# Moving the tiles of a float32r kernel within SBUF: moving tiles at one place modulo 512, gate and up weights 192 bytes below it

## What is computed

```python
def _swiglu(h, w_gate, w_up, w_down):
    return (jax.nn.silu(h @ w_gate) * (h @ w_up)) @ w_down     # 1024 -> 2816 -> 1024

x = x + 0.5 * _swiglu(_rmsnorm(x, g[0]), ffn_w_gate[layer, 0], ffn_w_up[layer, 0], ffn_w_down[layer, 0])
...
x = x + 0.5 * _swiglu(_rmsnorm(x, g[2]), ffn_w_gate[layer, 1], ffn_w_up[layer, 1], ffn_w_down[layer, 1])
```

## The kernel before

| tile | role | before | changed |
|---|---|---|---|
| `w_hi`, `w_lo`, `w_raw`, `xT`, `R` | weights of down and mixer products; state | 320 | 320 |
| `ffn_aH`, `ffn_aL` | moving, down products | 320 | 320 |
| `hH`, `hL` | moving, gate-up and mixer products | 64 | 320 |
| `st_hi`, `st_lo` | moving, gate-up | 448 | 320 |
| `tmp`, `ident`, `ones`, `bones` | scratch and constants | 448 | 320 |
| `gu_w_hi` 0, 1 | weights, gate-up | 384, 0 | 128, 128 |
| `gu_w_lo` 0, 1, 2 | weights, gate-up | 256, 384, 0 | 320, 128, 128 |
| `mixH`, `mixL`, `mH`, `mL`, `o_hi`, `o_lo`, `cq_hi`, `cv_hi` and other mixer tiles | moving | 64 | 320 |
| `yH`, `yL` and others of the first block | moving | 0 | 256 |
| `par`, `small` | columns of parameters | 320, 128 | 128, 224 |

## Time and profile before

### The profile page before, as it was taken

The page is one execution under the profiler, slowest core; times in us unless marked ns, Lnnn a source line. Parts: engine busy times, 40 slices in busy tenths (PEclk is TensorE's granted clock), DMA queues, the critical chain, the costliest instruction groups (busy, mean ns, idle before and its releaser), DMA issues.

```text
span 2411.5 us, 42260 instructions
## 1 busy us (share of the span) xinstructions
PE 2339.2 (97%) x16963; PEld 1986.4 (82%) x16963; DVE 1738.6 (72%) x2296; ACT 1144.1 (47%) x1758; POOL 880.0 (36%) x533
## 2 busy tenths in 40 slices
PE   8999989999999999988999999999999999999999
PEld 6667768789899777876898998998987557898997
DVE  7999986496486489765874867856856776883871
ACT  5533353465364346244662654643644344662552
POOL 3799944322313456422114133132134212114123
PEclk9999999999999999999999999999999999999999
DMA  5222214233343432002334343342333221233333
GB/s 151 79 79 79 75 57 127 74 88 100 104 115 90 111 90 74 27 3 58 111 95 118 106 114 89 88 131 77 114 88 100 52 58 53 81 101 107 106 89 96
DMA packets 420791, 214.48 MB, mean 89 GB/s; under 512 B 17317, under 2 KB 419035, under 8 KB 420603
## 3 DMA queue, kind: packets, MB, share of 16 engines
q1 hardware_dynamic: 416523, 209.05, 30.6%
q10 hardware_dynamic: 4080, 2.83, 0.5%
HBM read 209.22 MB, written 2.10 MB: 88 GB/s over the span
## 4 chain that ended last, share of the span: by engine, by line
PE 73%; DVE 17%; issue 3%; ACT 3%; POOL 3%; DMA 0%; ACTq 0%; DVEq 0%; POOLq 0%
PE bank L995 10%; PE bank L1000 10%; PE bank L1003 10%; PE bank L344 9%; PE bank L341 9%; PE bank L337 9%; DVE bank L1690 4%; PE bank L1863 2%; PE bank L1860 2%; PE bank L1856 2%; DVE gu_w_lo L592 1%; POOL w_lo L319 1%; PE bank L3400 1%; PE bank L2748 1%; DVE hL L368 1%
## 5 line engine op out<-in xcount | busy, mean ns | idle before, releaser
L319 POOL TENSOR_TENSOR w_lo<-w_raw,w_hi 128x1024 fp32r<-128x1024 f32 (+5 forms) x276 | 532.9, 1932 | 613.1 <-ACT w_hi L311 611.3
L311 ACT ACTIVATE w_hi<-w_raw 128x1024 fp32r<-128x1024 f32 (+5 forms) x276 | 237.6, 861 | 623.2 <-PE bank L344 468.7
L592 DVE TENSOR_TENSOR gu_w_lo<-gu_w,gu_w_hi 128x1024 fp32r<-128x1024 f32 (+1 forms) x256 | 364.9, 1428 | 90.6 <-ACT gu_w_hi L583 90.0
L664 POOL TENSOR_TENSOR ffn_aL<-tmp,ffn_aH 128x512 fp32r<-128x512 f32 x88 | 134.5, 1529 | 725.7 <-ACT ffn_aH L708 725.7
L583 ACT ACTIVATE gu_w_hi<-gu_w 128x1024 fp32r<-128x1024 f32 (+1 forms) x256 | 302.9, 1185 | 3.1 <-DVE gu_w L566 3.1
L995 PE MATMUL bank<-hH,gu_w_hi 128*128 128x256 f32 x1280 | 203.7, 281 | 5.0 <-ACT tmp L700 5.0
L1000 PE MATMUL bank<-hL,gu_w_hi 128*128 128x256 f32 x1280 | 200.7, 279 | 0.0
L1003 PE MATMUL bank<-hH,gu_w_lo 128*128 128x256 f32 x1280 | 200.3, 278 | 0.0
L700 ACT ACTIVATE tmp<-bank 128x256 f32<-128x256 f32 x320 | 120.8, 378 | 165.7 <-PE bank L1003 165.7
L968 DVE TENSOR_TENSOR bank<-bank,R 128x512 f32<-128x512 f32 x64 | 44.8, 699 | 204.1 <-PE bank L344 203.6
L337 PE MATMUL bank<-ffn_aH,w_hi 128*128 128x512 f32 x704 | 181.1, 390 | 0.0
(11 more groups left out here) (553 smaller groups left out, 4684.6 us busy)
## 6 DMA issues: line engine op xcount, KB each, us to landing
gu_w<-in_ffn_w_gate SPq DMA_DIRECT2D x88, 512.0 KB, 3.7
gu_w<-in_ffn_w_up SPq DMA_DIRECT2D x88, 512.0 KB, 4.8
w_raw<-in_w_in SPq DMA_DIRECT2D x48, 512.0 KB, 3.8
w_raw<-in_ffn_w_down SPq DMA_DIRECT2D x64, 384.0 KB, 3.4
w_raw<-in_ffn_w_down SPq DMA_DIRECT2D x64, 320.0 KB, 3.2
w_raw<-in_even_w_in SPq DMA_DIRECT2D x26, 512.0 KB, 3.9
w_raw<-in_w_conv_out SPq DMA_DIRECT2D x8, 512.0 KB, 3.9
w_raw<-in_w_out SPq DMA_DIRECT2D x8, 512.0 KB, 3.9
```

Source lines behind the costliest of these rows:

```text
L311: nc.scalar.activation(w_hi[u % 2][:, 0:K, :], w_raw[u % 4][:, 0:K, :], ACT.Identity).then_inc(w_hi_ready, 1)
L319: nc.gpsimd.tensor_tensor(w_lo[u % 2][:, 0:K, :], w_raw[u % 4][:, 0:K, :], w_hi[u % 2][:, 0:K, :].bitcast(F32), ALU.subtract).then_inc(w_l ...
L592: nc.vector.tensor_tensor(gu_wl[v % 3][:, b0:b1, :, :], gu_w[v % 3][:, b0:b1, :, :], gu_wh[v % 2][:, b0:b1, :, :].bitcast(F32), ALU.subtra ...
L664: nc.gpsimd.tensor_tensor(aL[:, in_half(n), :], up_t[:, :], aH[:, in_half(n), :].bitcast(F32), ALU.subtract).then_inc(a_lo, 1)
```

## The change

Only addresses change. Every engine's list of instructions is the same, in the same order, with the same shapes and waits (9941 rows over all engines when repeated ones are merged). `par` and `small` go to the front, so that `xT` starts at 320 and everything from `tmp` to `hH` follows without a gap; `place` always works modulo 512; the gate and up weights are put 192 bytes below the moving tiles instead of 64; `gu_w` 0 follows `hL` directly and so lies at the moving tiles' own place; `gu_w_hi` 0 is put ahead of the `st` tiles.

```diff
-            def place(self, r, step=256):
+            def place(self, r):
-                self.at += (r - self.at) % step
+                self.at += (r - self.at) % 512
                 return self.at
...
-        small = m.put("small", [P, 8])
-        m.place(64)
+        par = Map(m.at).put("par", [P, 408])
+        small = Map(m.at + 4 * 408).put("small", [P, 8])
+        m.at += 4 * 416
+        m.place(320)
         xT = m.put("xT", [P, DT, T])
...
-        par = m.put("par", [P, 416])
...
-        hH_at = m.place(ring_at)
-        GU_PLACE = hH_at - 64
+        hH_at = m.at
+        GU_PLACE = hH_at - 192
         hH = m.put("hH", [P, DT, T], F32R)
...
-        u_at = [f_map.place(GU_PLACE), 0, Map(ring_at).place(GU_PLACE)]
+        u_at = [f_map.at, 0, Map(ring_at).place(GU_PLACE)]
         f_map.put("gu_room0", [P, 7, 4, P])
-        f_map.place(hH_at)
         aH = f_map.put("ffn_aH", [P, GU, T], F32R)
         aL = f_map.put("ffn_aL", [P, GU, T], F32R)
-        u_at[1] = f_map.place(GU_PLACE, 128)
+        u_at[1] = f_map.place(GU_PLACE)
         f_map.put("gu_room1", [P, 7, 4, P])
...
+        gu_wh0 = f_map.put("gu_w_hi0", [P, 7, 4, P], F32R)
+        f_map.place(hH_at)
...
-        f_hi_at = f_map.place(hH_at, 128)
+        f_hi_at = f_map.at
```

More of the change, by code:

```diff
@@ L404, in build @@
         f_map = Map(ARENA)
-        u_at = [f_map.place(GU_PLACE), 0, Map(ring_at).place(GU_PLACE)]
+        u_at = [f_map.at, 0, Map(ring_at).place(GU_PLACE)]
         f_map.put("gu_room0", [P, 7, 4, P])
-        f_map.place(hH_at)
         aH = f_map.put("ffn_aH", [P, GU, T], F32R)
         aL = f_map.put("ffn_aL", [P, GU, T], F32R)
-        u_at[1] = f_map.place(GU_PLACE, 128)
+        u_at[1] = f_map.place(GU_PLACE)
         f_map.put("gu_room1", [P, 7, 4, P])
-        gu_w = [Map(at).put(f"gu_w{i}", [P, 7, 4, P]) for i, at in enumerate(u_at)]
-        gu_wl = [Map(at).put(f"gu_w_lo{i}", [P, 7, 4, P], F32R) for i, at in enumerate(u_at)]
-        gu_wh = [f_map.put("gu_w_hi0", [P, 7, 4, P], F32R), Map(Map(ring_hi_at).place(GU_PLACE)).put("gu_w_hi1", [P, 7, 4, P], F32R)]
+        gu_wh0 = f_map.put("gu_w_hi0", [P, 7, 4, P], F32R)
+        f_map.place(hH_at)
         st_hi, st_f, st_lo = [], [], []
-        f_hi_at = f_map.place(hH_at, 128)
+        f_hi_at = f_map.at
         for k in range(4):
@@ L425, in build @@
             st_f.append(f_lo_map.put(f"st_f{k}", [P, 3, HT]))
+        gu_w = [Map(at).put(f"gu_w{i}", [P, 7, 4, P]) for i, at in enumerate(u_at)]
+        gu_wl = [Map(at).put(f"gu_w_lo{i}", [P, 7, 4, P], F32R) for i, at in enumerate(u_at)]
+        gu_wh = [gu_wh0, Map(Map(ring_hi_at).place(GU_PLACE)).put("gu_w_hi1", [P, 7, 4, P], F32R)]
         hLf = Map(hH_at + 4 * DT * T).put("hL_f", [P, DT, T])
```

## The result

The changed kernel takes 2421.55 us (median of 6 runs, 2419.51 to 2426.09), the kernel before beside it 2412.06 (2410.85 to 2414.3): a ratio of 1.0035 with a 95% interval of 1.0025 to 1.0046. It is slower by 9.5 us. The prediction was 2393, a gain. What happened is rival 1 in the main, which had been priced at 2419.5.

A forecast was written before the change was run, and what follows sets the result against it. TensorE's pitch was taken to bound the kernel. Gain 21.7 - 0.8 - 1.7 = 19.2 us, giving 2394.1 from the profiled execution and 2392.4 from the median; predicted 2393 us, range 2389 to 2408.

The forecast's parts named there:

- rival 1: 256-wide gate-up matmuls: the slow pace is never shed, all 6720 run slow, 29.6 us instead of 21.7; 2419.5 us, chance 0.13.
- What bounds the kernel: Whole kernel: TensorE's pitch, busy 97% of the span; in second halves a mean of 116.6 ns from two paces.
- At constant places the pace persists: Gate-up units: with weights and moving operand at unchanged places, either pace (113.3 or 117.7 ns) continues; distance alone doesn't set it.
- The sum of the pace's cost, 21.7 us: All 256-wide matmuls: windows less their matmuls at 113.33 ns, 12.0 + 9.8, about 21.7 us to be gained before deductions.
- A change of the moving tile's place ends the fast pace: Borders of hH and st: the event, four times in a unit's seven products, would be gone with one moving place.
- The slow start of each of eight halves, until something ends it: 24 matmuls: Start of each feed-forward half: 24 matmuls slow by 4.4 ns, 0.1 us each, 0.8 us off the gain.
- Distance 0, bounds 0 and 3.3 us, taken at 1.7: Low-weight rounds of units v = 0, 3, 6, 9: between no cost and slow pace, half taken, 1.7 us off the gain.
- Rival 2: Units with low weights at distance 0 are slow throughout, the next without it fast again; 10.0 us stay, 2400.7 us, chance 0.20.
- There is room: Second halves: VectorE's 87.8 us fit into 104.7 us, 84%; the coming unit's low weights, next to be late, have room.
- Rival 4: VectorE or ScalarE takes the gain: ring of copies from PSUM binds, half the gain lost at most; 2402 us, chance 0.03.
- Plain units, mixer and down products unchanged: 512-wide matmuls: plain units taken at 0, bounds -1 and +1 us; mixer and down products keep their distance modulo 256, cost nothing.
- The rule of the SBUF — State Buffer page: TensorE's two independent read ports: a tile's place can't matter, sum 0, 2411.6 us; the prediction held the two paces against it.

The follow-up runs named there:

- run 1: Changed kernel with low buffer 0 at distance 64 too, so all gate and up weights at 64 from the one moving place: 2417.92 us.
- run 9: Changed kernel with all five weight buffers at distance 64 and the gated product earlier on VectorE: 2414.22 us, ratio 1.0006 to the kernel before.
- run 10: Changed kernel with all five weight buffers at distance 192 and the gated product earlier on VectorE: 2418.62 us, ratio 1.0023 to the kernel before.
- run 4: Changed kernel with the state sums (st tiles) alone 128 bytes off, so two moving places: 2412.15 us, ratio 1.0 to the kernel before.
- run 11: Changed kernel with high weights at distance 192, low ones at 64, and the gated product earlier on VectorE: 2395.67 us, ratio 0.9925 to the kernel before.
- run 8: Changed kernel with all five gate and up weight buffers at distance 0 from the one moving place: 2435.8 us, ratio 1.0097 to the kernel before.
- run 2: Changed kernel with one moving place kept but weights at the distances of the kernel before (high 64, 192; low 192, 64, 192): 2407.61 us.
- run 3: Changed kernel with both high weight buffers at distance 192 and all three low ones at 64: 2415.82 us, ratio 1.0015 to the kernel before.
- run 5: One moving place, weights at the distances of the kernel before, plus the gated product earlier on VectorE: 2391.09 us, ratio 0.991 to the kernel before.

## Why the prediction was wrong

- **What bounds the kernel: right.** The whole result lies in TensorE's pitch. Pace cost and gaps explain 8.6 of 9.5 us.
- **"At constant places the pace persists": right**, and too right. With all distances equal it persisted slow for 924 matmuls (runs 1, 9 and 10) and fast for 672 (run 9, units 69 to 76).
- **The sum of the pace's cost, 21.7 us: some 2.4 too high.** By the pitches the same windows hold 19.3 us of slow pace. The rest is mostly gaps between matmuls that the busy time of TensorE does not show, above all in the windows of 7 and 9 units (1.4 and 1.7 us of slow pace where I had 2.5 and 2.7).
- **"A change of the moving tile's place ends the fast pace": half of it.** The other half is that a step of the moving tile can also start the fast pace, where it takes the distance from 192 to 64 (run 4, and the counts there). This row was before me: the 12 matmuls on hH after st in unit 37 were fast after two or three, and no weight buffer changed its place there. I booked the event as a loss only. The change removes the loss and the cure.
- **"The slow start of each of eight halves, until something ends it: 24 matmuls", 0.8 us: the step that failed.** In the four second halves nothing in the changed kernel ends it: they are slow for all of their 924 matmuls, 4.3 us each where the term had 0.1. Run 1 shows the same without distance 0, and runs 9 and 11 show what was missing, a distance that goes from 192 to 64. With the first halves, the pace cost of the whole 256-wide work was 29.4 us where the sum left 2.5. Rival 1 named the mechanism, and its 0.13 was too low. I took unit 33's cure as a sign that short rounds at another distance cure, though the step there was from 192 to 64.
- **Distance 0, bounds 0 and 3.3 us, taken at 1.7: outside its bounds.** The upper bound was the slow pace, from rows at other distances. Rounds at distance 0 cost 120 ns, 6.7 above the floor, 27 x 28 x 6.7 = 5.1 us, and besides they end the fast pace (units 25 and 69). The analogy to 512-wide matmuls, which settle at their floor at distance 0, did not carry over to 256 columns (run 8). Rival 2 had "the next unit without it is fast again"; unit 25's half stayed slow.
- **"There is room" in VectorE's 84%: wrong**, though it did not decide here, since no second half got fast. It would have: run 2 kept 4.7 of some 20 us for this reason. The share of busy time did not show it; the order in two queues did. Rival 4 gave 2402 for this case; run 2 lost more than that.
- **Plain units, mixer and down products unchanged: right** within what I can tell. The plain units' 512-wide matmuls lost 0.3 us more than before (1.9 to 2.2), the down products 0.1 less.
- **The rule of the SBUF — State Buffer page** of the Trainium skill, "Who interferes with whom", with two independent read ports, would have made all these kernels alike. Runs 9 and 11 differ in the place of two buffers alone and in 18.6 us. The measurement decides: where the weights lie against the moving operand matters. These runs don't tell by what path.

**Open.** What the pace is a state of, I can't say. Nor why a step from 192 to 64 cures a half after down products but neither the slow stretches after a gap in run 3 and in unit 26 of run 11 nor units 4 to 10 in run 11, while the alternation of before's buffers (run 2) cures after gaps too.

## What to carry to other kernels

Before you remove an event that ends a good state, list what starts that state, and look whether the same event does. If the state has a memory, the cost of a layout is read from how its long stretches begin, not from a mean per border. And when TensorE gets 3% faster, follow the queue of each engine that frees its banks: 82% busy can be late in one place of every unit, and one instruction moved took run 2's 2407.6 us to run 5's 2391.1.

## What the runs showed of the hardware

- The pitch of a 128x256 fp32r matmul depends on the distance between weights and moving operand modulo 256 bytes: at 64 and 192 it is 113.3 or 117.7 ns, at 0 it is 120.0, and at 128 it was 120.0 in second halves and 117 to 119 in first ones.
- At 64 and 192 it is a state with memory. With all distances equal the slow pace lasted for 924 matmuls and the fast one for 672. A distance that goes from 192 to 64 can start the fast pace, a round at distance 0 or a step of the moving tile to another place ended it.
- A gap of 0.1 to 0.2 us ahead of one matmul can end the fast pace (P4 of unit 35 in runs 2 and 3). It need not (P4 of units 49 to 53 in run 1). It can start it too: in unit 4 of the changed kernel the first matmul of P3 began 258 ns after the one before it and the next one 229 ns later, and the slow pace was fast after them, until pitches of 257 and 226 ns at P4 of unit 5 made it slow again.
- The same layout holds either pace for a whole half. In run 9 units 47 to 54, after TensorE had waited 2.5 us in unit 46, were fast (pace cost of that half 0.2 us), and the four second halves, which follow down products without a wait, were slow (4.1 us each), with the same buffers at the same places. With all distances at 192 the same waits left the units slow (run 10).
- Behind that wait of 2.5 us in unit 46 the granted clock was at 1.2 GHz for some 3 us, and the pitch was 213 ns. The pace after it was the fast one in run 9 and the slow one in run 10, so the clock's fall alone does not set it either.
